# A two-layer decoder trunk: conv matrices, stores, reloads and transposes re-ordered, weight folding of layer 0 staged by head ahead of the convolution

## What is computed

```
for l in range(2):
    u = rms_norm(h, norm_mix_g[l])
    b_a, c_a, h_a, v_b, g_b = split(u @ w_in[l])              # 5 x 512 channels
    y_a = b_a * causal_dwconv3(c_a * h_a)
    y_b = silu(layer_norm(causal_dwconv31(v_b * sigmoid(g_b)) + bias))
    h = h + concat(y_a, y_b) @ w_out[l]
    h = h + cross_attention(rms_norm(h), rms_norm(mem))       # 4 heads, 256 memory tokens
    h = h + relu(rms_norm(h) @ w_up[l])**2 @ w_down[l]
out = rms_norm(h, final_g)
```

## Time and profile before

| | |
|---|---|
| median of 3 runs | 3399.99 us (3394.83 to 3403.18) |
| the profiled execution | 3395.3 us |
| its span, slowest core | 3393.7 us (others from 3381.2) |
| TensorE busy | 3227.1 us, 95% |
| VectorE, ScalarE, GpSimd busy | 1756.5, 1416.7, 716.7 us |
| chain that ended last | PE 84%, DMA 7%, DVE 3%, issue 3%, ACT 2% |

### The profile page before, as it was taken

How to read it: one execution, slowest core, us unless ns; L and a number is a source line. 1 busy time by engine, 2 the same in 40 slices (tenths; PEclk the granted TensorE clock), 3 DMA queues, 4 the chain that set the end, 5 groups by cost and what they waited for, 6 DMA issues and landing times.

```text
span 3393.7 us, 50732 instructions; the slowest of 8 cores (3381.2 to 3393.7 us)
## 1 busy us (share of the span) xinstructions
PE 3227.1 (95%) x15793; PEld 1550.6 (46%) x16080; DVE 1756.5 (52%) x3016; ACT 1416.7 (42%) x2821; POOL 716.7 (21%) x908
## 2 busy tenths in 40 slices
PE   5888999799998999999999999999999999999998
PEld 2535444444444444544444444454444544454443
DVE  6655324664366632574347743476436653257433
ACT  3444313563326531474333732256332653147421
POOL 1421003320033200340003400142003310034000
PEclk9999999899999999999999999999999999999999
DMA  5878744744565444444548344354456544444441
GB/s 118 170 166 152 125 77 80 182 75 75 114 174 128 77 76 78 98 119 85 100 89 221 81 79 79 83 141 75 76 115 176 124 78 79 78 101 106 78 79 57
DMA packets 135319, 361.95 MB, mean 107 GB/s; under 512 B 32272, under 2 KB 41744, under 8 KB 135056
## 3 DMA queue, kind: packets, MB, share of 16 engines
q0 software_dynamic: 64896, 222.86, 38.5%
q1 hardware_dynamic: 69616, 134.78, 12.5%
q10 hardware_dynamic: 544, 1.05, 0.1%
HBM read 521.68 MB, written 34.60 MB: 164 GB/s over the span
## 4 chain that ended last, share of the span: by engine, by line
PE 84%; DMA 7%; DVE 3%; issue 3%; ACT 2%; SPq 1%; POOL 0%; DVEq 0%; ACTq 0%; another core or an unknown queue 0%; POOLq 0%
PE ps L478 84%; DMA arena<-wts 2%; ACT arena L489 2%; DMA arena<-arena 2%; DMA wbf<-arena 1%; DVE arena L493 1%; DMA outT<-arena 1%; DVE arena L503 1%; DMA arena<-xT 1%; DVE arena L977 0%; SPq L814 0%; POOL arena L493 0%; DVE arena L499 0%; DVE arena L403 0%; ACT L517 0%
## 5 line engine op out<-in xcount | busy, mean ns | idle before, releaser
L478 PE MATMUL ps<-arena 128*128 128x512 bf16 (+2 forms) x15785 | 3225.8, 364 | 154.3 <-DMA arena<-arena 43.3
L478 PEld LDWEIGHTS ps<-arena 128*128 128x128 bf16 x16072 | 1549.8, 98 | 1829.3 <-issue 184.2
L493 DVE TENSOR_TENSOR arena<-arena 128x512 f32<-128x512 f32 (+1 forms) x1280 | 868.5, 689 | 708.9 <-ACT arena L489 691.8
L489 ACT ACTIVATE arena<-arena 128x512 bf16<-128x512 f32 (+5 forms) x1441 | 753.5, 575 | 1131.1 <-DVE arena L493 1069.8
L493 DVE TENSOR_TENSOR arena<-ps,arena 128x512 f32<-128x512 f32 (+1 forms) x448 | 306.5, 688 | 655.8 <-PE ps L478 587.5
L489 ACT ACTIVATE arena<-ps 128x512 f32<-128x512 f32 (+1 forms) x608 | 361.6, 595 | 618.7 <-PE ps L478 598.0
L442 POOL DMA_DIRECT2D arena<-wts x400 | 215.7, 540 | 1764.7 <-PE ps L478 1712.5
L489 ACT ACTIVATE arena<-ps,arena 128x256 f32<-128x256 f32 (+2 forms) x441 | 229.6, 535 | 181.1 <-DVE arena L499 78.9
L498 POOL TENSOR_SCALAR arena<-arena 128x256 bf16<-128x256 f32 (+1 forms) x176 | 220.3, 1255 | 284.9 <-DVE arena L493 102.7
L493 POOL TENSOR_TENSOR arena<-arena 128x512 f32<-128x512 f32 x128 | 172.2, 1352 | 346.5 <-ACT arena L489 191.1
L493 DVE TENSOR_TENSOR arena<-arena,ps 128x512 f32<-128x512 f32 x256 | 175.4, 685 | 98.1 <-PE ps L478 95.3
(11 more groups left out here) (14 smaller groups left out, 43.9 us busy)
## 6 DMA issues: line engine op xcount, KB each, us to landing
arena<-wts POOLq DMA_DIRECT2D x400, 512.0 KB, 5.5
arena<-wbf SPq DMA_DIRECT2D x64, 512.0 KB, 6.4
arena<-wbf SPq DMA_DIRECT2D x48, 576.0 KB, 4.4
arena<-xT SPq DMA_DIRECT2D x30, 512.0 KB, 5.7
outT<-arena SPq DMA_DIRECT2D x6, 2048.0 KB, 10.2
arena<-xT SPq DMA_DIRECT2D x6, 2048.0 KB, 11.7
wbf<-arena SPq DMA_DIRECT2D x16, 576.0 KB, 5.8
wbf<-arena SPq DMA_DIRECT2D x16, 512.0 KB, 10.1
```

Source lines behind the costliest of these rows:

```text
L478: ins = e.matmul(ps.ap, lhsT=l_, rhs=r_, start=(first and i == 0), stop=(last and i == n - 1))
L489: return e.activation(**kw)
L493: S.op(eng, lambda e: e.tensor_tensor(out=out.ap, in0=a.ap, in1=b.ap, op=op), reads=[a, b], writes=[out])
```

## The change

Six edits are made together.

1. `setup(0)` is called by `early()` between `ch_part(1)` and the convolution, where it stood behind projection B. The ring order follows, and in layer 0 `setup` calls `tick()` ahead of each of its 16 weights.
2. `prod` writes each head's products to one of two 8 KB staging halves by the head's parity (`stg`: the area of `cb`, the convolution's result, for layer 0; an area of its own for layer 1), and stores each head at once: two DMAs for the folded queries, in rows of 256 elements, and one for the folded values, in rows of 512. Six semaphores `sa` and `sw` stand for the six kinds by parity.
3. Builds are taken at every tick when there are any. The stores of convolution matrices during the convolution are gone.
4. `band_cast` copies `bands` of the next layer (now for both layers) from HBM to HBM with a cast, on GpSimd's queue, one every eighth tick of `ffn_up` in tile 0. Layer 1 of tile 0 therefore loads its matrices from `wbf`.
5. `final_apply` takes two channel blocks at a time and stores each pair (0.5 MB); the reloads, also 0.5 MB each, come behind all stores of both halves.
6. In `plan`, one score step is put ahead of transpose (0, 3), and transposes 4 to 7 move up to one step later.

```diff
-        stgA = [Buf(arena, U0, 4 * 2048, BF16, 2048), stgA1]
-        stgW = [Buf(arena, U0 + 16384, 4 * 2048, BF16, 2048), stgW1]
+        stg = [cb.off, stg1.off]
...
-            if builds and tick_no[0] > 6 and tick_no[0] % 2:
+            if builds:
                 builds.popleft()()
...
+                if ti == 0 and l == 0:
+                    seq += setup_order(0)
                 seq += [conv_id(ti, l, i) for i in range(8)]
                 seq += [w_id(l, C_B), w_id(l, C_B + 1)]
-                if ti == 0 and l == 0:
-                    seq += setup_order(0)
...
-        def wb_store(cid, src):
+        def band_cast(l, i):
+            cid = l * NWB_L + W_CONV + i
+            S.op("pool", lambda e: e.dma_start(out=wbf[cid], in_=bands[l * 8 + i]),
+                 writes=[piece(cid, 0, 4)], dma_sem=sem[f"bc{i}"])
             wb_ready.add(cid)
...
             def prod(hd):
                 b = kvt[hd % 2]
+                stA = Buf(arena, stg[l] + 8192 * (hd % 2), 2048, BF16, 1024)
+                stW = Buf(arena, stg[l] + 8192 * (hd % 2) + 4096, 2048, BF16, 512)
...
-                if hd % 2:
-                    for i in range(2):
-                        wb_store(l * NWB_L + W_AQ + hd - 1 + i, stA.c(hd - 1 + i))
+                hc = (hd % 2) * 256
+                for kh in range(2):
+                    cid = l * NWB_L + W_AQ + (hd // 2) * 2 + kh
+                    o = wbf[cid][:, 0:2048].rearrange("p (k c) -> p k c", c=512)[:, :, hc:hc + 256]
+                    i_ = stA.full[:, kh * 1024:(kh + 1) * 1024].rearrange("p (k c) -> p k c", c=256)
+                    S.op("sp", lambda e, o=o, i_=i_: e.dma_start(out=o, in_=i_), reads=[stA.c(kh)],
+                         writes=[piece(cid, hd % 2)], dma_sem=sem[f"sa{hd % 2}{kh}"])
...
+                c0 = l * NWB_L + W_VW
+                o = wbf[c0:c0 + 4, :, hd * 512:(hd + 1) * 512].rearrange("c p n -> p c n")
+                i_ = stW.full.rearrange("p (c n) -> p c n", n=512)
+                S.op("sp", lambda e, o=o, i_=i_: e.dma_start(out=o, in_=i_), reads=[stW.r()],
+                     writes=[piece(c0 + i, hd) for i in range(4)], dma_sem=sem[f"sw{hd % 2}"])
...
             ch_part(1)
+            early()
...
                 slot = ring_get(conv_id(ti, l, cc))
-                if ti == 0:
-                    wb_store(l * NWB_L + W_CONV + cc, slot.r())
...
             ring_free(2)
-            bgwork()
...
-                    (Sc, 0, 7), (Tr, 0, 3), (Sc, 1, 0), (Sc, 1, 1), (Tr, 0, 4), (Tr, 0, 5), (Sc, 1, 2), (Tr, 0, 6), (Tr, 0, 7),
-                    (Sc, 1, 3), (X, 0, 0), (Sc, 1, 4), (X, 0, 1), (Tr, 1, 0), (Sc, 1, 5), (X, 0, 2), (Tr, 1, 1), (Sc, 1, 6),
+                    (Sc, 0, 7), (Sc, 1, 0), (Tr, 0, 3), (Sc, 1, 1), (Sc, 1, 2), (Tr, 0, 4), (Tr, 0, 5), (Tr, 0, 6),
+                    (Sc, 1, 3), (Tr, 0, 7), (X, 0, 0), (Sc, 1, 4), (X, 0, 1), (Tr, 1, 0), (Sc, 1, 5), (X, 0, 2), (Tr, 1, 1), (Sc, 1, 6),
...
+                if ti == 0 and ntiles * nlayers > 1:
+                    for i in range(8):
+                        bg.append(lambda l=l, i=i: band_cast((l + 1) % nlayers, i))
+                        for _ in range(7):
+                            bg.append(lambda: None)
```

More of the change, by code:

```diff
@@ L229, in build_nc @@
         sem = {}
-        names = ["pe", "act", "dve", "pool", "spq", "misc", "xs0", "xs1", "xh0", "xh1", "o0", "o1", "st0", "st1", "mm0", "mm1"]
+        names = ["pe", "act", "dve", "pool", "spq", "misc", "xs0", "xs1", "st0", "st1", "mm0", "mm1"]
+        names += [f"bc{i}" for i in range(8)] + ["sa00", "sa01", "sa10", "sa11", "sw0", "sw1"]
         names += [f"xa{i}" for i in range(8)]
@@ L440, in ring_pump @@
                 elif kind != "b":
-                    n, src = (SLOT, bands[cid]) if kind == "c" else (2048, wts[cid])
-                    S.op("pool", lambda e, o=slot.full[:, 0:n], s=src: e.dma_start(out=o, in_=s),
+                    n = 2048
+                    S.op("pool", lambda e, o=slot.full[:, 0:n], s=wts[cid]: e.dma_start(out=o, in_=s),
                          reads=[h[1].r()] if 2 <= i < RING else [], writes=[slot.r(0, n)], dma_sem=sem[f"wc{i % RING}"])
@@ L448, in ring_pump @@
                     S.op("sp", lambda e, o=slot.full[:, 0:n], s=wbf[cid][:, 0:n]: e.dma_start(out=o, in_=s),
-                         reads=[Ref(None, "wbf", cid, cid + 1)], writes=[slot.r(0, n)], dma_sem=sem[f"w{i % RING}"])
+                         reads=[piece(cid, 0, 4)], writes=[slot.r(0, n)], dma_sem=sem[f"w{i % RING}"])
                 ring["loaded"] += 1
@@ L465, in ring_free @@
             ring_pump()
-        def wb_store(cid, src):
-            n = src.ap.shape[1]
-            S.op("sp", lambda e, o=wbf[cid][:, 0:n], s=src.ap: e.dma_start(out=o, in_=s),
-                 reads=[src], writes=[Ref(None, "wbf", cid, cid + 1)], dma_sem=sem[f"st{rot('st', range(2))}"])
+        def band_cast(l, i):
+            cid = l * NWB_L + W_CONV + i
+            S.op("pool", lambda e: e.dma_start(out=wbf[cid], in_=bands[l * 8 + i]),
+                 writes=[piece(cid, 0, 4)], dma_sem=sem[f"bc{i}"])
             wb_ready.add(cid)
@@ L683, in build_nc, with piece @@
                 bg.append(lambda l=l, c0=c0: mem_apply(l, c0))
+        def piece(cid, p, n=1):
+            return Ref(None, "wbf", cid * 4 + p, cid * 4 + p + n)
         def setup(l):
             finish_tasks()
-            stA, stW = stgA[l], stgW[l]
             def kv(hd):
                 for w, which in ((C_K, 0), (C_VP, 1)):
+                    if l == 0:
+                        tick()
                     slot = ring_get(w_id(l, w + hd))
@@ L728, in prod @@
                            [slot.r(0, 2048), b.r(512, 1024)])
-                        k = hd * 2 + mc
-                        base = dh * 4096 + k * 256
-                        o = stW.ref(stW.full[:, dh * 4096:(dh + 1) * 4096].rearrange("p (i r) -> p i r", r=2048)[:, :, k * 256:(k + 1) * 256],
-                                    base, base + 2048 + 256)
+                        o = stW.full[:, dh * 1024:(dh + 1) * 1024].rearrange("p (i r) -> p i r", r=512)[:, :, mc * 256:(mc + 1) * 256]
+                        o = stW.refs(o, [(dh * 1024 + i * 512 + mc * 256, dh * 1024 + i * 512 + (mc + 1) * 256) for i in range(2)])
                         i_ = Ref(ps.ap.rearrange("p (i c) -> p i c", c=256), "ps", ps.lo, ps.hi)
@@ L738, in prod @@
                 ring_free(1)
[L739 to L741 removed]
+                hc = (hd % 2) * 256
[5 more added lines that the diff above has]
+                         writes=[piece(cid, hd % 2)], dma_sem=sem[f"sa{hd % 2}{kh}"])
+                    if hd % 2:
+                        wb_ready.add(cid)
+                c0 = l * NWB_L + W_VW
[3 more added lines that the diff above has]
+                     writes=[piece(c0 + i, hd) for i in range(4)], dma_sem=sem[f"sw{hd % 2}"])
+                if hd == 3:
+                    for i in range(4):
+                        wb_ready.add(c0 + i)
             for hd in range(4):
@@ L747, in setup, with mixer @@
             prod(3)
-            for i in range(4):
-                wb_store(l * NWB_L + W_VW + i, stW.c(i))
-        def mixer(l, ti, lz, bgwork):
+        def mixer(l, ti, lz, early):
             vb = l * NV_L
@@ L1076, in one, with pair @@
                 stt("dve", h[s].c(c), h[s].c(c), vcol(V_FINAL + c), RC[s].r(), ALU.mult, ALU.mult, extra_reads=[vref])
-            for c in range(8):
-                bg.append(lambda c=c: one(c))
-            bg.append(lambda: final_store(ti, s))
+            def pair(i):
+                one(2 * i)
+                one(2 * i + 1)
+                final_store(ti, s, i)
+            for i in range(4):
+                bg.append(lambda i=i: pair(i))
+                if i % 2:
+                    bg.append(lambda: None)
+            if s == NS - 1:
+                for z in range(NS):
+                    for i in range(4):
+                        bg.append(lambda z=z, i=i: reload(ti, z, i))
         lz = first_lz
@@ L1136, in build_nc @@
         drain_bg()
-        S.wait_all("sp", [sem["o0"], sem["o1"]] + [sem[f"oc{i}{j}"] for i in range(NS) for j in range(4)])
+        S.wait_all("sp", [sem[f"oc{i}{j}"] for i in range(NS) for j in range(4)])
         with nc.Block() as block:
```

45 lines of the change are left out of this document (21 added, 24 removed).

## The result

The changed kernel takes 3361.6 us (median of 4 runs, 3358.7 to 3363.5), the kernel before 3398.4 beside it: ratio 0.989, 95% interval 0.9873 to 0.9907, that is 37 us less (32 to 43). The forecast was 3350 us, 3330 to 3376. Any of these kernels has executions that run some per cent longer at a lower granted clock on one die or both; the times and ratios here leave them out. The profiled execution took 3360.9 us, its span 3359.4.

The account below looks back on a forecast made before the run. TensorE, busy 95% of the span, bounds the kernel; its waits decide. Terms -31.7 - 20 - 27 + 30 = -49 us on 3395.3 give 3346, 3351 for the median; stated 3350 us, range 3330 to 3376.

Parts of the forecast that it names:

- turns of tiles 1 to 3: Waits at the next tile's layer 0 convolution go, as reloads no longer stand ahead of its input DMAs; gain 31.7 us.
- layer 1 of tile 0, matrices: Without the matrix stores on SyncE, the 17.0 us wait for `ycat` and 3 us of slow clock go; gain 20 us.
- layer 0 of tile 0: Four terms for projections, convolution wait, `setup(0)` and late convolution results; sum -27 us, bounds -36 and -12.
- stores by head in `setup(1)`: Small pieces each wait for a load packet's turn, holding copies, PSUM banks and TensorE; cost 30 us, bounds 0 and 45.
- transposes, casts: Moved attention transposes cost 0, bounds -5 and +5; casts in tile 0's FFN cost 0 while covered, bound 5.
- rival D: Casts from HBM to HBM spread badly over the engines, making the kernel slower than before; 3450 us at c = 22; chance 0.03.
- (a): Layer 0 of tile 0: builds leave the projections, so 8.2 us of VectorE waits and 1.5 of slow clock go; -9.7.
- (c): `setup(0)`, with weights loaded early, takes 39 us instead of 58, nine weights being paced by VectorE's builds and copies; -19.
- (d): Layer 0 of tile 0: the convolution's results wait for the head stores; +6 us, bounds 0 and 20.
- (b): Layer 0 of tile 0: the 3.9 us wait at the convolution goes; -3.9, bounds 0 and -5.
- Rival A: Head stores hide, as queues serve in larger turns or loads run out sooner; `setup(1)` and (d) cost 0; 3315; chance 0.24.

Follow-up runs that it names:

- matrices_alone: Kernel before, with only the stores of convolution matrices replaced by casts from HBM to HBM in tile 0's feed-forward part; ratio 0.9919, 27.5 us faster.
- turn_and_matrices: Kernel before, with both the paired stores and reloads at the turn of a tile and the casts in place of the matrices' stores; 3342.8 us, ratio 0.9859.
- fill_for_builds: Changed kernel, with the eight VectorE builds of layer 0's convolution matrices in tile 0 replaced by fills with zeros; ratio 0.9891.
- stage4_rows2k: Changed kernel, with a staging place for each head in both layers and query products stored in pieces of 2 KB; 3322.7 us, ratio 0.9791.

## Why the prediction was near, and where it was off

The sum was -49 us, the measurement -37. The time lies inside the range, nearer than the terms are, since two gains were put too high and the loss too:

| term | predicted | measured, from |
|---|---|---|
| turns of tiles 1 to 3 | -31.7 | -24.9 by the periods, -26 undone, -23 alone |
| layer 1 of tile 0, matrices | -20 | -19.4, period of `matrices_alone` |
| layer 0 of tile 0 | -27 | -16.6, of which -7.5 are the matrices' stores |
| stores by head in `setup(1)` | +30 | +25.0, against `turn_and_matrices` |
| transposes, casts | 0 | 0 |

The measured terms add up to -36.

**Turns: the mechanism right, the size 6 us off.** The prediction took back the waits of all three turns and "2.9 after it: the convolution restarts at the lower clock" for each, less 1 us a tile for VectorE. The three turns had lost 33.3 us against the other periods, of which 24.9 came back: a turn takes 399.4 to 401.2 us, where the prediction wanted one near 398. Of the 3.6 us that the first one takes more than the other periods, 1.5 are the `ycat` wait at 1045.7 and about 1 is a lower clock. The window 985 to 1012 us after the change is granted 0.96 with TensorE busy all of it (0.84 to 990 us, 0.94 to 995, then 1.00):

```profile
985.00:1012.00 27.00, 27.00 (x142) 13.90 (x141) 17.80 (x35) 8.51 (x21) 15.62 (x20) 0.96 0.70 199
```

**Layer 1 of tile 0: right**, to the microsecond where the stores alone go. The casts are hidden, as priced; rival D falls.

**Layer 0 of tile 0: this step failed by 10 us.** (a) holds: the 8.2 us of waits in the projections are gone, the clock in 53 to 113 us is 1.00 (before, 0.97). (c) said 39 us for `setup(0)` because VectorE's builds pace it. Its first weight follows the projections at about 94 us, the convolution starts at 137.8: 44 us, and with 3.3 us less VectorE work `fill_for_builds` wins 0.7. What is late there is the loads (5.9 us of TensorE's waits), and the copies behind the head stores (ScalarE waits 8.2 us for a store at 130.0). The prediction had heads 0 and 1 landing in time. How much each of the two adds is known only for the stores, some 3 us. (d) said 6 us for the layer norm; it is 8.6 (up to 11.9 in the other traces), with the same mechanism: ScalarE waits for a head store at 160.15 and VectorE for ScalarE. In `stage4_rows2k`, where both are gone, the mark lies 11.8 us earlier (238.86). The four terms that can be read off add to about -18: waits of the projections and clock -9, (b) -4, `setup(0)` -14, layer norm +9.

**Stores by head: right, 2 to 5 us too high.** One q0 packet for each q1 packet was taken from the 901 to 901 of the earlier trace rows, and it held in every window in which neither queue ran out: 1060 to 1060, 1221 to 1221, 1137 to 1136, 1508 to 1506. The prediction's landings, 308, 322 and 339 us, are in the times of the kernel before; less the 16.6 us gained ahead of them they are 291, 305 and 322. Measured: 296.7, 309.7, 322.6. The steps are 13 us, not 14 and 17, and TensorE's waits sum up to 26.6 us where it had 29.

Rival A, that the head stores hide, is refuted: copies wait for stores that land 13.0 us apart. Whether the queues take turns packet by packet is another question, which equal counts over 26 us don't answer, since two queues served in equal groups would show them too; the prediction did not say so. Two windows of 1 us in the changed kernel, 300 to 301 and 304 to 305, answer it:

```profile
q0 software_dynamic: 40, 0.16, 99.1%
q1 hardware_dynamic: 40, 0.02, 10.0%
...
q0 software_dynamic: 35, 0.14, 84.4%
q1 hardware_dynamic: 35, 0.02, 8.8%
```

In 1 us each of the 16 engines moves two or three packets of either queue on average. In all eight windows of 1 us from 298 to 306 us the two counts differ by at most 2. By the rule of the Trainium skill (DMA: Bandwidth & Descriptors, "Queues, rings and completion order"), about 9 to 17 descriptors of one queue before the engine turns, a group of loads would last 9 x 0.41 = 3.7 us or more (an estimate). In 1 us an engine would then serve mostly one queue, and the two counts would agree only if the engines' turns happened to cancel out each time. The trace does not agree with it: in both windows the turn is one by one.

The prediction's working from this rule was wrong too. It gave a head's 96 pieces 6 to 11 turns and "some 5 us", and so the 3315 us of rival A. But between two turns of q1 an engine would serve a group of loads. With groups of the same size in both queues that is 11 turns of 3.7 us or 6 of 7.0 us, some 40 us, an estimate that is the same as one by one gives (96 x 0.41 = 39 us). For the time of this kernel the two don't differ; the rule would have given the forecast.

What stays open: the 2 to 4 us left at each turn are read, not tried, and so is the 1.3 us by which the other three periods grew.

## What to carry to other kernels

A store in many small pieces beside a queue of big loads is paid in turns, not in bytes: count its packets per engine, times the time of one load packet, for as long as loads are queued, and ask first what waits for its landing. To shorten it helps only where nothing else is handed the wait: more staging alone (in layer 1) gave nothing, larger pieces alone gave nothing, both gave 34 us. And a gain is best taken apart: the -37 us are 48 gained by two edits and 11 to 15 given back by the rest. As they stand, those two alone make the better kernel (3342.8 us against 3361.6); with four places and pieces of 2 KB the whole change does (3322.7).

## What the runs showed that was not expected

SyncE's own issue took long while small pieces were queued beside loads. Its queue in the changed kernel, 280 to 330 us (start, length):

```profile
280.36 0.36 SPq L752 DMA_DIRECT2D wbf<-arena  x1
284.72 20.14 SPq L745 DMA_DIRECT2D wbf<-arena  x2
305.01 12.63 SPq L752 DMA_DIRECT2D wbf<-arena  x1
```

An issue that took 0.36 us at 280.4 took 12.6 us for one and 20.1 us for two, so everything behind it on SyncE was late as well. No run was made to find out what holds it. When the loads are gone, the same queue is fast: between 120 and 135 us q1 moved 3712 packets, 2.36 MB, in 15 us.

The granted clock fell to 0.84 (985 to 990 us of the changed kernel) in a stretch in which TensorE had been busy without a gap, and from 995 us on it was 1.00 again. Nothing in the trace says why.
